# A two-layer decoder step on one core: first four weight units worked in halves, high-part products ahead, the next three units in idle banks, and GpSimd's squares after the low parts of x

## Chip, cores and metric

One core of a Trainium2 chip runs the whole step as one program. The metric is device time in microseconds; lower is better. Three runs of the kernel before had a median of 1188.85 us (1187.78 to 1189.05).

## What is computed

The reference is one inference step of a decoder trunk of two layers for 256 prompt rows and 8 decode rows (264 columns side by side, `N`). The change touches only the first matrix product of the first layer, `swiglu(rmsnorm(x), wi, wo)`:

```python
def rmsnorm(x, g):
    y = xf * lax.rsqrt(jnp.mean(xf * xf, axis=-1, keepdims=True) + EPS)
    return (y * g).astype(x.dtype)

def swiglu(x, wi, wo):
    gt, up = jnp.split(x @ wi, 2, axis=-1)
    return (jax.nn.silu(gt) * up) @ wo

x = x + 0.5 * swiglu(rmsnorm(x, w['ffn1_norm'][i]), w['ffn1_wi'][i], w['ffn1_wo'][i])
```

After it follow a Mamba-2 mixer, further SwiGLU blocks, shared K/V, window attention and gated embeddings, all through the same weight stream.

## The kernel before

**Units.** All weights are cut into units of 128x1024 fp32 (512 KB), numbered from 0 through the whole network, which go through a ring of four slots (`RING`). For each unit SP loads `raw`, ScalarE (ACT) copies it to `whi` in fp32r (the high part), VectorE (DVE) subtracts to get `wlo` (the low part), and TensorE (PE) makes for each of the unit's 8 tiles three products into one PSUM bank, `split_products`: `whi` by `xh`, `whi` by `xl`, `wlo` by `xh`, so 24 matmuls of 128x264 a unit. `xh` and `xl` are the high and low part of the input times the gain, one tile of each for every 128 rows of the model. The row factor 1/rms isn't in them: DVE multiplies it in when it takes a finished bank (`take`, L1623), after the squares of x have been summed (`sums`, L544, a plain fp32 matmul), rooted on ACT (`root`, L1154) and inverted on DVE (L1617, `row_factor`).

**What orders the work.** Each engine has its own program, written out by hand, and waits on counting semaphores: `first_hi`, `hi_ready`, `first_lo`, `lo_ready` (halves and units split), `xh_ready`, `xl_ready` (tiles of x), `unit_used` (units that PE has finished, four ahead at the start), `a_free` (banks that DVE has taken, also four ahead), `first_part` and `first_sum` (sums of squares of GpSimd and DVE). SP loads unit u into its slot only when `lo_ready` shows that unit u - 4 has been split. ACT splits unit u + 4 only when `unit_used` shows that unit u has been used. So of a slow step in one engine, everything queued behind it is late too.

**The beginning, stage `f1i0`.** PE runs 30 matmuls on zeros (`warm_up`, L504). x comes in four pairs of tiles (`x_pair`), units 0 and 1 in halves (four tiles each), units 2 and 3 whole. PE works units 0 and 1 side by side two tiles at a time, each tile with all its three products, then unit 2, the sums, unit 3. From unit 4 on each unit waits for its bank out of four (`unit_a`). GpSimd (POOL) squares three tiles of x and adds them as soon as x lands, ACT squares the other five (L1136), DVE adds those (L1794) and joins both (L1796). SP loads units 2 and 3, then, behind `lo_ready`, units 4 and 5, three tables (`cs`, `convs`, `vs`: 802.5, 384 and 143 KB), and units 6 and 7. The rest of the stage is a loop of four units a turn, in which `gate` and `up` take banks, ACT makes `silu`, and `hidden`, `round_h` and `low_h` make the high and low part of the hidden tile.

Of the kernel before, what the change touches and what calls it, by code (L numbers as in the profile page):

```python
# [22 lines left out]
P = 128  # L23
# [16 lines left out]
WARM = 30  # L40
# [90 lines left out]


# [36 lines left out]
def trunk_kernel(nc, weights, xT, g1, pT, cst, vec, convst, ssm0, kcT, vc_in, ck, cv,  # L169
# [3 lines left out]
    with ExitStack() as ctx:  # L173
# [77 lines left out]
        half_landed = [sem(f"half_landed{s}") for s in range(2)]  # L251
# [193 lines left out]
        def _(sp):  # L445
            sp.dma_start(gain0, g1).then_inc(gain_landed, 16)
            for h in range(4):
                sp.dma_start(x[:, 2 * h:2 * h + 2, :], xT[:, 2 * h:2 * h + 2, :]).then_inc(x_pair[h], 16)
                if h == 0:
                    for u in range(2):  # L450
                        sp.dma_start(raw[:, u, 0:HALF], weights[u, :, 0:HALF]).then_inc(half_landed[u], 16)
                if h == 1:
                    for u in range(2):
                        sp.dma_start(raw[:, u, HALF:UNIT], weights[u, :, HALF:UNIT]).then_inc(raw_landed[u], 16)
            for u in range(2, 2 * RING):
                if u >= RING:
                    sp.wait_ge(lo_ready, u - RING + 1)
# [39 lines left out]
        def _(pe):  # L497
# [78 lines left out]
            def first_units(stage, b_wait, rh=xh, rl=xl):  # L576

                if stage == "f1i0":
                    pe.wait_ge(a_free, A0[stage] + 2)
                    for h in range(KT // 2):  # L580
                        for j in range(2):
                            if h == 0:
                                pe.wait_ge(first_lo, j + 1)
                            if h == KT // 4:
                                pe.wait_ge(lo_ready, j + 1)
                            for k in (2 * h, 2 * h + 1):
                                pe.wait_ge(xl_ready, XREADY[stage] + k + 1)
                                mm = split_products(bank[j][:, 0:N], j, k, rh[:, k, :], rl[:, k, :], k == 0, k == KT - 1)
                    mm.then_inc(unit_used, 2)
                    unit_a(stage, 0, 2)  # L590
                    sums(stage)
                    unit_a(stage, 0, 3)
                    return
# [3 lines left out]
                for j in (2, 3):  # L597
                    unit_a(stage, 0, j, b_wait, rh=rh, rl=rl)

# [381 lines left out]
            ffn_in("f1i0", None)  # L981
# [109 lines left out]
        def _(act):  # L1091
# [64 lines left out]
            def ffn_in(stage, out, ffn, aside=None, late_work=False, spread=None):  # L1156
# [9 lines left out]
                if stage == "f1i0":  # L1166
# [3 lines left out]
                    act.preload_act_table(ACT.Silu)  # L1170
                else:
# [5 lines left out]
                ahead(stage, 0, 2)  # L1177
                round_h(0, 0)
                silu(0, 1)
                ahead(stage, 0, 3)  # L1180
# [56 lines left out]
            for m in range(KT):  # L1237
                if m % 2 == 0:
                    act.wait_ge(x_pair[m // 2], 16)
                act.activation(xh[:, m, :], x[:, m, :], ACT.Copy, scale=gain0[:, m:m + 1]).then_inc(xh_ready, 1)  # L1240
                if m == 1:
                    for u in range(2):
                        act.wait_ge(half_landed[u], 16)
                        act.activation(whi[:, u, 0:HALF], raw[:, u, 0:HALF], ACT.Copy).then_inc(first_hi, 1)
                if m == 3:
                    for u in range(2):
                        act.wait_ge(raw_landed[u], 16)
                        act.activation(whi[:, u, HALF:UNIT], raw[:, u, HALF:UNIT], ACT.Copy).then_inc(hi_ready, 1)
            round_unit(*unit(0, 0, 2))
            for m in range(POOL_SQUARES, KT):  # L1250
                square_x(m)
            round_unit(*unit(0, 0, 3))
# [317 lines left out]
        def _(dve):  # L1570
# [48 lines left out]
            def take(dst, stage, j, i=0):  # L1619

                dve.wait_ge(unit_used, U0[stage] + j + 4 * i + 1 + RING)
                src = bank[sin_bank(j) if stage == "sin" else QUERY_BANK[j] if stage == "q" else (A0[stage] + j) % 4]
                dve.tensor_tensor(dst, src[:, 0:N], rstd[:, :], ALU.mult).then_inc(a_free, 1)  # L1623

            def ffn_in(stage, out, ffn, aside=None, late_groups=0, spread=None):
# [16 lines left out]
                if stage == "f1i0":  # L1642
                    ahead(stage, 0, 0)
                row_factor(stage)
# [4 lines left out]
                ahead(stage, 0, 1)  # L1649
# [35 lines left out]
                with dve.Fori(SPREAD_AT[-1] + 1 if late_groups else 1, 2 * FT // RING) as i:  # L1685
# [90 lines left out]
            for m in range(KT):  # L1776
                if m % 2 == 0:
                    dve.wait_ge(x_pair[m // 2], 16)
                dve.wait_ge(xh_ready, m + 1)
                dve.scalar_tensor_tensor(out=xl[:, m, :], in0=x[:, m, :], scalar=gain0[:, m:m + 1], in1=xh[:, m, :].bitcast(F32),  # L1780
                                         op0=ALU.mult, op1=ALU.subtract).then_inc(xl_ready, 1)
                if m == 1:
                    for u in range(2):
                        dve.wait_ge(first_hi, u + 1)
                        dve.tensor_tensor(wlo[:, u, 0:HALF], raw[:, u, 0:HALF], whi[:, u, 0:HALF].bitcast(F32), ALU.subtract).then_inc(first_lo, 1)
                if m == 3:
                    for u in range(2):
                        dve.wait_ge(hi_ready, u + 1)
# [790 lines left out]
```

## Time and profile before

| | us |
|---|---|
| median of 3 runs | 1188.85 |
| lowest, highest | 1187.78, 1189.05 |
| the profiled execution's own time | 1188.74 |
| its span in the trace | 1186.9 |
| PE busy | 1174.9 (99%) |
| DVE busy | 866.4 (73%) |
| ACT busy | 698.7 (59%) |
| POOL busy | 246.2 (21%) |

The span is what the trace covers; the time of a run is 1.84 us more in this execution. A row of a timeline has the start in us from the span's start, the busy time, the engine and the operation, and in brackets how long the engine had been idle ahead of it and what ended that. "x2" is two instructions merged in one row.

### The profile page before, as it was taken

How to read it: one execution, taken by the hardware profiler on the slowest of the kernel's cores; microseconds unless marked ns; L12 is line 12 of the kernel's file. 1: busy time of each engine (PE TensorE's matmuls, PEld its weight loads, DVE VectorE, ACT ScalarE, POOL GpSimd, SP SyncE). 2: the span in 40 equal slices, each digit the busy share in tenths (PEclk: the TensorE clock that was granted, in tenths of full speed). 3: DMA queues.
4: the chain of work that ended last, by engine and by line, in shares of the span. 5: the costliest groups of instructions: out<-in, count | busy, mean ns of one | idle time of the engine just before them, and what ended most of it. 6: DMA issues, size and time to landing. Idle time of an engine off the chain costs nothing.

```text
span 1186.9 us, 26623 instructions
## 1 busy us (share of the span) xinstructions
PE 1174.9 (99%) x9823; PEld 1153.3 (97%) x9823; DVE 866.4 (73%) x1377; ACT 698.7 (59%) x1149; POOL 246.2 (21%) x352
## 2 busy tenths in 40 slices
PE   9999999999999999999999999999999999999998
PEld 8999999999999899999999999999999899999998
DVE  7766645999899858767745987788468777776447
ACT  6445435777786747555546765555368765444345
POOL 1000001422221202122344333232026310000001
PEclk9999999999999999999999999999999999999999
DMA  8765554755445375866886677656743346555552
GB/s 288 253 205 181 183 184 143 256 180 202 162 157 193 113 220 179 329 214 247 283 299 232 213 269 280 226 166 237 261 150 108 106 163 209 186 184 178 179 181 86
DMA packets 63297, 239.90 MB, mean 202 GB/s; under 512 B 7672, under 2 KB 9632, under 8 KB 58848
## 3 DMA queue, kind: packets, MB, share of 16 engines
q1 hardware_dynamic: 56880, 197.83, 49.8%
q0 software_dynamic: 6064, 40.66, 9.4%
q8 instruction: 41, 0.67, 0.2%
q10 hardware_dynamic: 288, 0.54, 0.2%
q14 instruction: 24, 0.20, 0.0%
HBM read 226.87 MB, written 13.39 MB: 202 GB/s over the span
## 4 chain that ended last, share of the span: by engine, by line
PE 87%; DVE 7%; ACT 3%; DMA 2%; issue 1%; POOL 0%; SPq 0%; DVEq 0%; ACTq 0%; POOLq 0%
PE bank L509 28%; PE bank L510 27%; PE bank L511 27%; DVE wlo L1576 1%; DMA raw<-weights 1%; DVE xact L1850 1%; DMA xact<-stat_rows 1%; ACT whi L1098 1%; DVE xl L1595 1%; PE bank L881 1%; PE bank L907 0%; PE bank L886 0%; ACT under L1494 0%; PE bank L687 0%; DVE zs L1976 0%
## 5 line engine op out<-in xcount | busy, mean ns | idle before, releaser
L1576 DVE TENSOR_TENSOR wlo<-raw,whi 128x1024 fp32r<-128x1024 f32 x367 | 456.0, 1246 | 236.9 <-ACT whi L1098 235.5
L509 PE MATMUL bank<-xh,whi 128*128 128x264 f32 x2008 | 576.5, 287 | 1.9 <-DVE zs L1623 0.8
L510 PE MATMUL bank<-xl,whi 128*128 128x264 f32 x2008 | 569.6, 284 | 0.0
L511 PE MATMUL bank<-xh,wlo 128*128 128x264 f32 x2008 | 569.3, 284 | 0.0
L1098 ACT ACTIVATE whi<-raw 128x1024 fp32r<-128x1024 f32 x367 | 385.5, 1054 | 242.4 <-PE bank L511 225.1
L509 PEld LDWEIGHTS bank<-xh,whi 128*128 128x128 f32 x2008 | 378.6, 189 | 5.0 <-DVE wlo L1576 1.8
L510 PEld LDWEIGHTS bank<-xl,whi 128*128 128x128 f32 x2008 | 378.8, 189 | 0.8
L511 PEld LDWEIGHTS bank<-xh,wlo 128*128 128x128 f32 x2008 | 376.9, 188 | 0.0
L509 PE MATMUL bank<-hh,whi 128*128 (+1 forms) x896 | 255.9, 286 | 1.8 <-DVE hl L1960 1.7
L511 PE MATMUL bank<-hh,wlo 128*128 (+1 forms) x896 | 255.0, 285 | 0.0
L510 PE MATMUL bank<-hl,whi 128*128 (+1 forms) x896 | 254.7, 284 | 0.0
L509 PEld LDWEIGHTS bank<-hh,whi 128*128 128x128 f32 x896 | 169.2, 189 | 2.7 <-issue 2.1
L510 PEld LDWEIGHTS bank<-hl,whi 128*128 128x128 f32 x896 | 169.1, 189 | 0.1
L511 PEld LDWEIGHTS bank<-hh,wlo 128*128 128x128 f32 x896 | 168.8, 188 | 0.0
L1164 ACT ACTIVATE hh<-gu 128x264 fp32r<-128x264 f32 (+1 forms) x88 | 37.4, 425 | 168.3 <-DVE gu L1635 168.3
L2204 POOL TENSOR_TENSOR sq<-sq 128x264 f32<-128x264 f32 x49 | 39.6, 808 | 448.4 <-ACT sq L1136 443.1
L1623 DVE TENSOR_TENSOR gu<-bank,rstd 128x264 f32<-128x264 f32 x192 | 82.1, 429 | 15.3 <-PE bank L511 12.8
L1640 DVE TENSOR_TENSOR hl<-gu,hh 128x264 f32 (+1 forms) x88 | 41.5, 472 | 28.7 <-ACT hh L1164 28.7
L2354 POOL TENSOR_TENSOR xact<-xact,da_bc 128x512 f32<-128x512 f32 x32 | 38.7, 1210 | 100.8 <-PE bank L511 100.8
L1850 DVE SCALAR_TENSOR_TENSOR xact<-under,vs,xact 128x256 f32<-128x256 f32 x96 | 47.3, 493 | 2.3
L1635 DVE TENSOR_TENSOR gu<-gu 128x264 f32<-128x264 f32 x88 | 44.1, 502 | 0.0
L2359 POOL TENSOR_TENSOR xact<-xact 128x512 f32<-128x512 f32 x20 | 29.1, 1457 | 59.9 <-PE bank L511 56.2
(335 smaller groups left out, 1007.2 us busy)
## 6 DMA issues: line engine op xcount, KB each, us to landing
raw<-weights SPq DMA_DIRECT2D x367, 512.0 KB, 3.5
under<-ssm POOLq DMA_DIRECT2D x8, 1024.0 KB, 7.1
xact<-ssm POOLq DMA_DIRECT2D x8, 1024.0 KB, 7.4
out_ssm_s<-xact POOLq DMA_DIRECT2D x8, 1024.0 KB, 6.0
xact<-dtx_rows POOLq DMA_DIRECT2D x5, 1024.0 KB, 10.7
zs<-dtx_rows POOLq DMA_DIRECT2D x2, 1024.0 KB, 14.1
x<-xT SPq DMA_DIRECT2D x4, 264.0 KB, 5.6
xact<-stat_rows POOLq DMA_DIRECT2D x2, 528.0 KB, 7.5
```

The costliest lines, as they stand in the source:

```text
L509: pe.matmul(out, whi[:, w, c], rh, start=start, stop=False)
L510: pe.matmul(out, whi[:, w, c], rl, start=False, stop=False)
L511: return pe.matmul(out, wlo[:, w, c], rh, start=False, stop=stop)
L1098: act.activation(whi[:, s, :], raw[:, s, :], ACT.Copy).then_inc(hi_ready, 1)
L1164: act.activation(dst, gu[:, 2 * p + 1, :], ACT.Copy).then_inc(hh_ready, 1)
L1576: dve.tensor_tensor(wlo[:, s, :], raw[:, s, :], whi[:, s, :].bitcast(F32), ALU.subtract).then_inc(lo_ready, 1)
L1623: dve.tensor_tensor(dst, src[:, 0:N], rstd[:, :], ALU.mult).then_inc(a_free, 1)
L1635: dve.tensor_tensor(gu[:, 2 * p + 1, :], gu[:, 2 * p, :], gu[:, 2 * p + 1, :], ALU.mult).then_inc(h_ready, 1)
L1640: dve.tensor_tensor(one(hl), gu[:, 2 * p + 1, :], one(hh).bitcast(F32), ALU.subtract).then_inc(hl_ready, 1)
L1850: dve.scalar_tensor_tensor(out=out, in0=xr[:, k:k + T], scalar=vs[:, V_CW + CT * k + c:V_CW + CT * k + c + 1], in1=out, op0=ALU.mult, op1= ...
L2204: pool.tensor_tensor(sq3[:, 0, :], sq3[:, 0, :], sq3[:, m, :], ALU.add).then_inc(sq_pair, 1)
L2354: pool.tensor_tensor(by_head(part), by_head(part), da_bc[:, 2 * k:2 * k + 2, 4 * q:4 * q + 4].unsqueeze(3).to_broadcast([P, 2, 4, 64]), AL ...
```

## The change

The first four units are all loaded, split and multiplied in halves, in this order: for tiles 0 to 3, units 0 and 1 two tiles at a time in turn, then units 2 and 3 four tiles each; then the same for tiles 4 to 7. Within such a piece (`first_piece`) PE makes all products of the high weights with `xh`, then those with `xl`, then those of the low weights, and waits only for what each of them reads. The sums come after unit 3. Units 4, 5 and 6 go to banks 5, 6 and 7, which are idle at this time (`first_bank`), without a wait for a taken bank; unit 7 waits for all four first banks. GpSimd's squares wait for all eight tiles of `xl`. The warming products are 22, not 30. ACT splits unit 6 ahead of the first `silu` and unit 7 ahead of the second. The first turn of PE's and DVE's loop is written out.

```diff
-WARM = 30
+WARM = 22
+def first_bank(n):
+    return n + 1 if 4 <= n < 7 else n % 4
...
+            load_x(0)
+            load_half(0, 0)
+            load_half(1, 0)
+            load_x(1)
+            load_half(2, 0)
+            load_half(3, 0)
+            load_x(2)
+            load_half(0, 1)
+            load_x(3)
+            for u in range(1, RING):
+                load_half(u, 1)
+            for u in range(RING, 2 * RING):
+                sp.wait_ge(lo_ready, u - RING + 1)
                 sp.dma_start(raw[:, u % RING, :], weights[u]).then_inc(raw_landed[u % RING], 16)
...
+            def first_piece(j, k0, n):
+                tiles = range(k0, k0 + n)
+                at = lambda k: slice(k * P, k * P + P)
+                for k in tiles:
+                    if k0 < KT // 2:
+                        pe.wait_ge(first_hi, j + 1)
+                    else:
+                        pe.wait_ge(hi_ready, j + 1)
+                    pe.wait_ge(xh_ready, k + 1)
+                    pe.matmul(bank[j][:, 0:N], whi[:, j, at(k)], xh[:, k, :], start=k == 0, stop=False)
+                for k in tiles:
+                    pe.wait_ge(xl_ready, k + 1)
+                    pe.matmul(bank[j][:, 0:N], whi[:, j, at(k)], xl[:, k, :], start=False, stop=False)
+                if k0 < KT // 2:
+                    pe.wait_ge(first_lo, j + 1)
+                else:
+                    pe.wait_ge(lo_ready, j + 1)
+                for k in tiles:
+                    mm = pe.matmul(bank[j][:, 0:N], wlo[:, j, at(k)], xh[:, k, :], start=False, stop=k == KT - 1)
...
+            def first_network():
+                pe.wait_ge(a_free, RING)
+                for half in range(2):
+                    k0 = half * KT // 2
+                    for k in (k0, k0 + 2):
+                        for j in range(2):
+                            first_piece(j, k, 2)
+                    for j in (2, 3):
+                        first_piece(j, k0, 4)
+                sums("f1i0")
+                for n in range(RING, 2 * RING):
+                    pe.wait_ge(lo_ready, n + 1)
+                    if n == 2 * RING - 1:
+                        pe.wait_ge(a_free, n + 1)
+                    for k in range(KT):
+                        mm = split_products(bank[first_bank(n)][:, 0:N], n % RING, k, ...)
+                    mm.then_inc(unit_used, 1)
...
+                    ahead(stage, 0, 2)
                 silu(0, 0)
-                ahead(stage, 0, 2)
+                ahead(stage, 0, 3 if stage == "f1i0" else 2)
...
+            low_half(0, 1)
+            low_half(1, 1)
+            low_pair(3)
+            low_half(2, 1)
+            low_half(3, 1)
...
             pool.memset(eps0, EPS)
+            pool.wait_ge(xl_ready, KT)
```

**DVE, from the split of tiles 4 and 5 of x to the reciprocal.** `wlo` 128x512 is half a unit, 128x1024 a whole one; `sq` is the chain of the squares. Before:

```order
L1780 SCALAR_TENSOR_TENSOR xl<-x,under,xh 128x264 [waits xh_ready,x_pair3]
L1780 SCALAR_TENSOR_TENSOR xl<-x,under,xh 128x264 [waits xh_ready]
L1576 TENSOR_TENSOR wlo<-raw,whi 128x1024 [waits hi_ready]
L1794 TENSOR_TENSOR sq<-sq 128x264 [waits sq_ready]
L1794 TENSOR_TENSOR sq<-sq 128x264 [waits sq_ready,dve_step] x3
L1796 TENSOR_TENSOR sq<-sq 128x264 [waits first_part,dve_step]
L1576 TENSOR_TENSOR wlo<-raw,whi 128x1024 [waits hi_ready] x2
L1617 RECIPROCAL rstd<-rstd 128x264 [waits std_ready]
```

And now:

```order
L1848 TENSOR_TENSOR wlo<-raw,whi 128x512 [waits hi_ready] x2
L1841 SCALAR_TENSOR_TENSOR xl<-x,under,xh 128x264 [waits xh_ready,x_pair3]
L1841 SCALAR_TENSOR_TENSOR xl<-x,under,xh 128x264 [waits xh_ready]
L1848 TENSOR_TENSOR wlo<-raw,whi 128x512 [waits hi_ready] x2
L1865 TENSOR_TENSOR sq<-sq 128x264 [waits sq_ready]
L1865 TENSOR_TENSOR sq<-sq 128x264 [waits sq_ready,dve_step] x3
L1867 TENSOR_TENSOR sq<-sq 128x264 [waits first_part,dve_step]
L1632 TENSOR_TENSOR wlo<-raw,whi 128x1024 [waits hi_ready] x2
L1673 RECIPROCAL rstd<-rstd 128x264 [waits std_ready]
```

The last two tiles of `xl` now stand behind two halves of `wlo`, and the two whole units behind the sum of squares are units 4 and 5, where they were 3 and 4.

**ACT, from the root to the second `silu`** (L1098 and L1143 split a unit, L1159 and L1204 are `silu`). Before:

```order
L1154 ACTIVATE rstd<-bank,under 128x264 [waits sums_done]
L1170 ACT_TABLE_LOAD
L1159 ACTIVATE gu<-gu 128x264 [waits a_free]
L1098 ACTIVATE whi<-raw 128x1024 [waits unit_used,raw_landed2]
L1164 ACTIVATE hh<-gu 128x264 [waits h_ready]
L1159 ACTIVATE gu<-gu 128x264 [waits a_free]
```

And now:

```order
L1199 ACTIVATE rstd<-bank,under 128x264 [waits sums_done]
L1215 ACT_TABLE_LOAD
L1143 ACTIVATE whi<-raw 128x1024 [waits unit_used,raw_landed2]
L1204 ACTIVATE gu<-gu 128x264 [waits a_free]
L1143 ACTIVATE whi<-raw 128x1024 [waits unit_used,raw_landed3]
L1209 ACTIVATE hh<-gu 128x264 [waits h_ready]
L1204 ACTIVATE gu<-gu 128x264 [waits a_free]
```

The split of unit 6, with its wait for the landing of unit 6, has moved ahead of the first `silu`.

**SP, up to the loop.** Now (before, the first wait for `lo_ready` stood behind the eleventh transfer, now behind the thirteenth, and what follows it is unchanged):

```order
L459 DMA raw<-weights 128x512 x3
L474 DMA raw<-weights 128x1024 [waits lo_ready] x2
L476 DMA cs<-cst 128x1605
L477 DMA zs<-convst 128x768
L478 DMA vs<-vec 128x286
L474 DMA raw<-weights 128x1024 [waits lo_ready] x2
```

What has moved is how far DVE must be for unit 4's load: `lo_ready` counts unit 0 only when its second half is split.

## Rows read from the trace of the kernel before

**Rows 1.** The page: span, busy time of PE, chain that ended last.

```profile
span 1186.9 us, 26623 instructions
PE 1174.9 (99%) x9823; PEld 1153.3 (97%) x9823; DVE 866.4 (73%) x1377; ACT 698.7 (59%) x1149; POOL 246.2 (21%) x352
PE 87%; DVE 7%; ACT 3%; DMA 2%; issue 1%; POOL 0%; SPq 0%; DVEq 0%; ACTq 0%; POOLq 0%
```

**Rows 2.** Stretches of PE: length, busy (products), granted clock, DMA share, GB/s.

```profile
7.66:17.96 10.30, 9.58 (x75) 1.00 0.96 349
17.96:21.66 3.70, 3.52 (x28) 1.00 1.03 404
21.66:24.56 2.90, 2.90 (x24) 1.00 0.62 218
30.36:1182.40 1152.04, 1146.41 (x9626) 1.00 0.59 200
```

**Rows 3.** Timeline of PE: warming, first product, sums, unit 4.

```profile
1.28 6.54 PE L504 MATMUL bank<-hh 128*128 128x264 f32 x30 [1.28 <-DVE hh L1774]
7.66 0.28 PE L509 MATMUL bank<-xh,whi 128*128 128x264 f32 x1
17.96 0.61 PE L544 MATMUL bank<-sq,under 128*128 128x264 f32 x2
21.66 0.36 PE L509 MATMUL bank<-xh,whi 128*128 128x264 f32 x1 [0.18 <-DVE gu L1623]
```

**Rows 4.** Pieces of the chain that ended last: start, us, what.

```profile
2.12 5.08 DMA raw<-weights
8.55 1.72 DVE xl L1780 x2
11.50 6.26 DMA raw<-weights
```

**Rows 5.** Timeline of ACT.

```profile
5.02 0.61 ACT L1244 ACTIVATE whi<-raw 128x512 fp32r<-128x512 f32 x1
7.22 0.63 ACT L1244 ACTIVATE whi<-raw 128x512 fp32r<-128x512 f32 x1 [1.59 <-DMA raw<-weights]
7.93 0.92 ACT L1240 ACTIVATE xh<-x,under 128x264 fp32r<-128x264 f32 x2
11.87 1.06 ACT L1098 ACTIVATE whi<-raw 128x1024 fp32r<-128x1024 f32 x1 [0.20 <-DMA raw<-weights]
16.55 1.06 ACT L1098 ACTIVATE whi<-raw 128x1024 fp32r<-128x1024 f32 x1 [1.10 <-DMA raw<-weights]
21.55 0.42 ACT L1159 ACTIVATE gu<-gu 128x264 f32<-128x264 f32 x1 [1.03 <-DVE gu L1623]
22.59 1.06 ACT L1098 ACTIVATE whi<-raw 128x1024 fp32r<-128x1024 f32 x1 [0.61 <-DMA raw<-weights]
```

**Rows 6.** Timeline of DVE.

```profile
4.85 1.85 DVE L1780 SCALAR_TENSOR_TENSOR xl<-x,under,xh 128x264 fp32r<-128x264 f32 x2 [3.62 <-ACT xh L1240]
6.62 0.68 DVE L1785 TENSOR_TENSOR wlo<-raw,whi 128x512 fp32r<-128x512 f32 x1
11.39 1.69 DVE L1780 SCALAR_TENSOR_TENSOR xl<-x,under,xh 128x264 fp32r<-128x264 f32 x4
14.15 1.82 DVE L1794 TENSOR_TENSOR sq<-sq 128x264 f32<-128x264 f32 x4
21.77 1.21 DVE L1576 TENSOR_TENSOR wlo<-raw,whi 128x1024 fp32r<-128x1024 f32 x1
```

**Rows 7.** Timelines of POOL and SP.

```profile
4.18 1.33 POOL L2211 TENSOR_TENSOR sq<-x 128x264 f32<-128x264 f32 x2 [3.21 <-DMA x<-xT]
5.59 0.82 POOL L2213 TENSOR_TENSOR sq<-sq 128x264 f32<-128x264 f32 x1
10.90 0.93 SPq L458 DMA_DIRECT2D raw<-weights  x2
14.29 3.64 SPq L458 DMA_DIRECT2D raw<-weights  x2
```

More of the change, by code:

```diff
@@ L250, in trunk_kernel @@
         x_pair = [sem(f"x_pair{h}") for h in range(4)]
-        half_landed = [sem(f"half_landed{s}") for s in range(2)]
+        half_landed = [sem(f"half_landed{s}") for s in range(RING)]
         first_hi = sem("first_hi")
@@ L576, in first_units @@
             def first_units(stage, b_wait, rh=xh, rl=xl):
[L578 to L593, printed above, removed]
                 unit_pair(stage, b_wait, stage != "f1i1", rh, rl)
@@ L598, in first_units @@
                     unit_a(stage, 0, j, b_wait, rh=rh, rl=rl)
+            def first_piece(j, k0, n):
[17 more added lines that the diff above has]
+                    mm = pe.matmul(bank[j][:, 0:N], wlo[:, j, at(k)], xh[:, k, :], start=False, stop=k == KT - 1)
+                if k == KT - 1:
+                    mm.then_inc(unit_used, 1)
[14 more added lines that the diff above has]
+                    for k in range(KT):
+                        mm = split_products(bank[first_bank(n)][:, 0:N], n % RING, k, xh[:, k, :], xl[:, k, :], k == 0, k == KT - 1)
+                    mm.then_inc(unit_used, 1)
+                with pe.Fori(2, 2 * FT // RING) as i:
+                    for j in range(RING):
+                        unit_a("f1i0", i, j)
             def first_units_p(stage, b_wait):
@@ L980, in _ @@
             warm_up()
[L981 removed]
+            first_network()
             stage_b("f1o0", FT, "sin")
@@ L1236, in _, with high_pair, high_half @@
             act.wait_ge(gain_landed, 16)
[L1237 to L1249, printed above, removed]
+            def high_pair(h):
+                act.wait_ge(x_pair[h], 16)
+                for m in (2 * h, 2 * h + 1):
+                    act.activation(xh[:, m, :], x[:, m, :], ACT.Copy, scale=gain0[:, m:m + 1]).then_inc(xh_ready, 1)
+            def high_half(u, h):
+                c = slice(h * HALF, h * HALF + HALF)
+                act.wait_ge(raw_landed[u] if h else half_landed[u], 16)
+                act.activation(whi[:, u, c], raw[:, u, c], ACT.Copy).then_inc(hi_ready if h else first_hi, 1)
+            high_pair(0)
+            high_half(0, 0)
+            high_half(1, 0)
+            high_pair(1)
+            high_half(2, 0)
+            high_half(3, 0)
+            high_pair(2)
+            high_half(0, 1)
+            high_pair(3)
+            for u in range(1, RING):
+                high_half(u, 1)
             for m in range(POOL_SQUARES, KT):
                 square_x(m)
-            round_unit(*unit(0, 0, 3))
             ffn_in("f1i0", "f1o0", 0)
@@ L1621, in take @@
                 dve.wait_ge(unit_used, U0[stage] + j + 4 * i + 1 + RING)
-                src = bank[sin_bank(j) if stage == "sin" else QUERY_BANK[j] if stage == "q" else (A0[stage] + j) % 4]
+                src = bank[sin_bank(j) if stage == "sin" else QUERY_BANK[j] if stage == "q" else
+                           first_bank(4 * i + j) if stage == "f1i0" and isinstance(i, int) else (A0[stage] + j) % 4]
                 dve.tensor_tensor(dst, src[:, 0:N], rstd[:, :], ALU.mult).then_inc(a_free, 1)
@@ L1643, in ffn_in @@
                     ahead(stage, 0, 0)
+                    ahead(stage, 0, 1)
                 row_factor(stage)
@@ L1648, in ffn_in @@
                     ahead(stage, 0, 0)
-                ahead(stage, 0, 1)
+                    ahead(stage, 0, 1)
                 hidden(0, 0)
```

54 lines of the change are left out of this document (26 added, 28 removed).

## Prediction

> **What bounds the kernel now.** I read the page first, for what the end hangs on: PE is busy 1174.9 of 1186.9 us and carries 87% of the chain that ended last [rows 1]. Then PE in stretches. From unit 4 on 24 products take 2.90 us, 0.121 us each, and from 30.36 to 1182.4 PE is busy 1146.41 of 1152.04 us [rows 2]. So behind the beginning nothing is to be had or lost by this change except as a shift: if unit n starts d earlier, where n is the first unit that no longer waits, the end comes d earlier. The whole question is what PE does ahead of that unit.
>
> Of PE's first 27 us: 30 warming products from 1.28 to about 7.66, then the first real product; the sums at 17.96, when 72 products (3 units) are done; unit 4 at 21.66 [rows 3]. 72 products at 0.121 are 8.7 us, and the stretch took 10.3, so 1.6 us are holes. From 17.96 to 21.66 stand the sums and unit 3's 24 products: 2.9 of 3.7 us, so 0.8 us for sums and the wait of unit 4 for its bank. What made the holes is in the chain [rows 4]: the load of unit 1's first half (ends 7.2), a pair of `xl` on DVE, and the load of unit 5 (ends 17.76), behind whose split on ACT the root is queued, and behind that the reciprocal. DVE and the transfers feed PE here, not PE itself.
>
> **Part 1, an earlier first product.** 22 warming products at 0.218 (6.54/30 [rows 3]) end at 1.28 + 4.8 = 6.1 us. Unit 0's first half is split at 5.02 + 0.61 [rows 5], so PE goes on at 6.1. Its first piece has six products; its last two want `wlo`, which DVE has at about 6.4: GpSimd no longer runs beside the first `xl` pair, and that pair cost 1.85 us beside it, 0.85 alone (half of 1.69 for four) [rows 6, 7]. The six end at 6.1 + 6 x 0.218 = 7.4. Then unit 1's first half is wanted, which lands at 7.2 and is split by 7.85 [rows 5]. So 0.5 us of hole, and the price of earlier start is bounded by a transfer: 12 products are done at about 8.9 (unit 1's low half at 8.6).
>
> Loads ahead: unit 1's half lands at 7.2 and unit 2 at 11.85 [rows 5], with 264, 256, 256, 264, 264 and 512 KB between, 0.66 us for each quarter MB. In the new order the pieces land at 7.9 (x pair 1), 8.55, 9.2 (units 2 and 3), 9.9, 10.5 (unit 0), 11.2 (x pair 3), 11.85, 12.5, 13.1 (units 1 to 3). ACT (0.61 a half, 0.46 an x tile) splits the second halves by 11.4, 13.0, 13.6 and 14.2. DVE (0.68 a half) has them by 12.1, 13.7, 15.2 and 15.9, with the last `xl` pair between the second and the third, at 14.5 [rows 5, 6]. PE, which from 9.3 on has 12 products of each unit's half ready to run, makes units 2 and 3's first halves until 13.4 and reaches each of the other pieces just after its `wlo`: unit 3 ends at 19.2. Before, it started at 18.21 and ended at 21.2. That is 2.0 us earlier, of which the sums, now behind it, take back 0.25 to 0.44.
>
> **Part 2, the sum of squares becomes late.** GpSimd starts at about 14.4. Its three squares (0.67 to 1.02; I take 0.7) and two additions (0.82) [rows 7] end at 18.3. DVE has two halves of `wlo` (1.36) and four additions (1.82 [rows 6]) in this time: 3.1 us alone. Alone, it waits for GpSimd until 18.3, joins at 18.7, and the sums at 19.2 wait for nothing. At the rate of the first `xl` pair beside GpSimd (half) it does 2.0 of 3.1 by 18.3, the rest by 19.4, joins by 19.8; sums 20.2. Behind the join DVE makes unit 4's `wlo` (1.21 [rows 6]): 19.9 or 21.0, and unit 4 starts at 20.0 or 21.1, against 21.66. These are the ends, gain 1.6 and 0.55; I take 21.1, since both GpSimd and DVE have two operands from SBUF here as in the row.
>
> The Trainium skill (GPSIMD Engine Reference, the table at its top) says that GpSimd shares its SBUF interfaces with VectorE and that instructions with two SBUF inputs contend; by that rule the move takes the cost away from `xl` and lays it on the chain of squares. The row of the first pair agrees.
>
> **Part 3, unit 6.** Here is what I think decides. Unit 4's load waits for unit 0's second low half: 12.1, where it was issued at 10.9 [rows 7]; unit 5's for unit 1's at 13.7 (11.5 [rows 4]); the three tables (1.33 MB) and unit 6's load stand behind it on SP. Unit 6 landed at 22.59, 4.8 us behind unit 5 [rows 4, 5]. If all is later as issued, unit 6 lands 1.3 later, 23.9; if the engines are full anyway, as late as before, 22.6. Unit 4's load took 5.6 us though the queue was draining, so mostly the issue counts: I take 23.5. Now ACT holds the first `silu` behind unit 6's split. From the landing: split 1.06, `silu` 0.42, `hidden` and `gate` on DVE 0.8, `wlo` of unit 6 1.21 [rows 5, 6], so 3.5 us and 0.1 to PE: 27.1 (26.2 to 27.5). The other bound for unit 6 is unit 4's start plus two units: 26.9 (25.8). Before, it started at 21.66 + 5.8 = 27.46. So the gain that remains is about 0.35 us (0 to 1.6). What the idle banks save (0.18 idle and the slower start of the row at 21.66, about 0.4) is in these numbers: unit 4 doesn't wait for the reciprocal any more.
>
> Behind unit 6: unit 7 lands 1.25 later, is split at about 26, needs four taken banks (DVE at 28) and its `wlo` (29.3), and PE wants it at 30.0: covered by 0.7 us. The unrolled turns, the banks and the later `k_old` transfer lie beside PE and cost nothing while that cover lasts.
>
> **The sum.** 1186.9 - 0.35 = 1186.55 of span, and 1.84 around it: 1188.4 for the profiled execution, which stood 0.11 below the median of 1188.85. So 1188.5.
>
> **Rivals.** (A) *Data and DVE come early.* The load that ended at 7.2 had been issued at 2.12 and took 5.08 us [rows 4], 0.7 us being what such a piece needs. If it lands at 6, as its size would allow, all pieces follow 0.7 to 1.2 earlier, and DVE isn't slowed in the squares: unit 4 starts at 19 to 19.8, unit 6 at 24.8 to 25.6, 1.9 to 2.7 us earlier: 1186.2 to 1187.0. Against it: before would be no such gainer, its first product being bound by the warming, and the row of contention is plain.
>
> (B) *Nothing remains*: unit 6 lands at 23.9 or later, `silu` late, 27.5 or more: 1188.9 to 1189.6.
>
> (C) *Slower: the clock.* The warming ran at 0.218 a product, 264 columns at 1.2 GHz, until shortly before 7.66, and products run at 0.121, 2.4 GHz, behind it [rows 2, 3]; what PE had done was run without a hole for some 6 us. Now there is a hole of 0.5 us at 7.4. If it holds the rise off, each product costs 0.1 more. The first 12 are hidden by the feed. The sums' lateness hides 0.6 us, and unit 6's some more, so 15 slow products cost about nothing; from 40 slow products on (4.0 less 1.0 hidden, less 0.35 gained) it is over 1191.2. For it: nothing in the trace but the moment. Against: the holes of 0.5 and 0.3 us at 8 to 12 us left the clock at 1.00 [rows 2]. The Trainium skill (TensorE: Matmul & The Clock Gate, Part 1) says that the gate follows recent activity and that the moment of the rise varies between runs. By that rule a rise at about 8 us would be possible in this kernel too and would cost under 1 us, mostly hidden.
>
> **How the numbers follow.** A measurement of this kernel tells about 0.2%, 2.4 us, from no change. Forecast (gain 0 to 1.6) 0.56, (A) 0.22, (B) 0.16, (C) 0.06. Of (A) I count three quarters as over 2.4 us, since median runs differ by 0.6 either way and the feed may be better than I can read: faster 0.17, same 0.76, slower 0.07. The range takes (A)'s end and (B)'s with that 0.6: 1186.0 to 1190.0.
>
> **What would show it.** In the trace of the changed kernel: first product at 6.1; a hole at 7.4; `xl` tiles at 0.42; unit 3 done near 19.2; the join of squares at 18.7 to 19.8 and unit 4's start behind a `wlo`, not behind `gu`; ACT waiting for unit 6's transfer ahead of the first `silu`; unit 6's start at 27.1. I am wrong if unit 6 starts before 26 (its landing or the contention misjudged), or if the shift of unit 6 isn't the shift of the end.

## Result and the profile after

Over 22 runs each the changed kernel has a median of 1191.11 us (1189.02 to 1194.33), the kernel before 1189.09 (1187.78 to 1192.23): 2.0 us longer, ratio 1.0017, 95% interval 1.0011 to 1.0023. 14 of the 22 lie over 1190.5 us, of the kernel before 2 of 22. The forecast was 1188.5 in a range to 1190.0, so both sign and range failed.

The page of the changed kernel (first part, PE's line, chain by engine), to be read against [rows 1]:

```profile
span 1189.4 us, 26619 instructions
PE 1175.5 (99%) x9815; PEld 1153.7 (97%) x9815; DVE 869.1 (73%) x1379; ACT 698.8 (59%) x1151; POOL 247.7 (21%) x352
PE 86%; DVE 6%; ACT 3%; DMA 2%; issue 1%; SPq 0%; POOL 0%; DVEq 0%; ACTq 0%; POOLq 0%
```

It is bound as before; 2.5 us of span have come in somewhere. First the beginning, PE's timeline, then DVE's, then ACT's (against [rows 3, 5, 6]):

```profile
6.29 0.42 PE L610 MATMUL bank<-xh,whi 128*128 128x264 f32 x1
19.76 0.71 PE L560 MATMUL bank<-sq,under 128*128 128x264 f32 x2 [0.90 <-DVE sq L1867]
20.90 0.39 PE L525 MATMUL bank<-xh,whi 128*128 128x264 f32 x1 [0.42 <-DVE wlo L1632]
27.76 0.39 PE L525 MATMUL bank<-xh,whi 128*128 128x264 f32 x1 [0.78 <-DVE wlo L1632]
```

```profile
4.61 0.90 DVE L1841 SCALAR_TENSOR_TENSOR xl<-x,under,xh 128x264 fp32r<-128x264 f32 x2 [3.38 <-ACT xh L1288]
15.80 3.44 DVE L1865 TENSOR_TENSOR sq<-sq 128x264 f32<-128x264 f32 x4
19.27 0.43 DVE L1867 TENSOR_TENSOR sq<-sq 128x264 f32<-128x264 f32 x1
21.93 1.80 DVE L1673 RECIPROCAL rstd<-rstd 128x264 f32<-128x264 f32 x1
26.49 1.22 DVE L1632 TENSOR_TENSOR wlo<-raw,whi 128x1024 fp32r<-128x1024 f32 x1
```

```profile
19.70 1.06 ACT L1143 ACTIVATE whi<-raw 128x1024 fp32r<-128x1024 f32 x1 [3.00 <-DMA raw<-weights]
24.39 1.06 ACT L1143 ACTIVATE whi<-raw 128x1024 fp32r<-128x1024 f32 x1 [1.96 <-DMA raw<-weights]
25.36 0.40 ACT L1204 ACTIVATE gu<-gu 128x264 f32<-128x264 f32 x1
```

The first product comes at 6.29, not 7.66; unit 4 at 20.90, 0.8 us earlier than before. But unit 5 lands at 19.7, where it landed at 17.8 [rows 4], and unit 6 at 24.4, where it landed at 22.6 [rows 5]. Behind that landing stand its split, the first `silu`, `hidden`, `gate` and `wlo` at 26.49, and PE has unit 6 at 27.76, with 0.78 us of hole. The kernel before started it two units behind 21.66 [rows 3], at 27.56 in its trace. So at unit 6 the changed kernel is 0.2 us *behind*, from unit 7 on 0.3 (the first product behind a hole takes 0.1 longer, 0.39 for 0.28), and this 0.3 stays to 425 us.

The next two places are far from the change. The chain that ended last around 414 us, changed kernel, then kernel before, and the wait of PE behind it in the changed kernel (1.7 us in the kernel before):

```profile
414.42 10.11 DMA xact<-stat_rows
```

```profile
414.06 9.50 DMA xact<-stat_rows
```

```profile
PE bank L525 <- DVE hl L2030: 2.3, 1, 2.3
```

The mixer's group norm sends its row factors through memory and reads them back to all partitions (`stat_rows`). PE has other tiles to work on meanwhile, runs out of them, and stands until DVE has the ninth tile's low part. This hole has grown by 0.65 us. Then stretches of PE around the attention stage (length, busy, products, granted clock, DMA), changed kernel:

```profile
939.00:942.37 3.37, 3.12 (x74) 1.00 0.00 0
942.37:945.78 3.41, 3.41 (x23) 0.50 0.48 159
945.78:949.20 3.42, 3.42 (x30) 1.00 0.50 157
```

and what PE did ahead of it:

```profile
941.30 1.10 PE L778 MATMUL bank<-small,xact 128*64 128x4 f32 x32
```

Behind 32 products of four columns the clock fell from 2.4 to 1.2 GHz for 3.41 us: 1.2 us later from there on. The kernel before has 1.00 in these stretches. With 0.3 (beginning), 0.65 (hole), 0.1 (between 440 and 700 us), 1.2 (clock) and 0.2 (around the last sum of squares, at 1166 us) the 2.5 us of span are all placed. What runs had to tell was whether the last four belong to the change or to one execution.

### The profile page after: what moved, and what is told of

It is laid out like the page before. It is cut to its first block, busy times and chain, and to the rows that moved or that the text cites. A ratio compares the mean times of both kernels' runs of the same rounds, so it can differ in the third digit from the quotient of the medians.

```text
span 1189.4 us, 26619 instructions
## 1 busy us (share of the span) xinstructions
PE 1175.5 (99%) x9815; PEld 1153.7 (97%) x9815; DVE 869.1 (73%) x1379; ACT 698.8 (59%) x1151; POOL 247.7 (21%) x352
## 4 chain that ended last, share of the span: by engine, by line
PE 86%; DVE 6%; ACT 3%; DMA 2%; issue 1%; SPq 0%; POOL 0%; DVEq 0%; ACTq 0%; POOLq 0%
PE bank L525 27%; PE bank L526 27%; PE bank L527 27%; DVE wlo L1632 1%; DMA xact<-stat_rows 1%; DVE xact L1920 1%; DMA raw<-weights 1%; ACT whi L1143 1%; DVE xl L1651 1%; PE bank L926 1%; DMA x<-xT 0%; PE bank L952 0%; PE bank L931 0%; ACT under L1550 0%; PE bank L732 0%
## 5 line engine op out<-in xcount | busy, mean ns | idle before, releaser
L525 PE MATMUL bank<-xh,whi 128*128 128x264 f32 x1976 | 566.5, 287 | 2.2 <-DVE wlo L1632 1.4
L526 PE MATMUL bank<-xl,whi 128*128 128x264 f32 x1976 | 560.2, 283 | 0.0
L527 PE MATMUL bank<-xh,wlo 128*128 128x264 f32 x1976 | 559.7, 283 | 0.0
L1143 ACT ACTIVATE whi<-raw 128x1024 fp32r<-128x1024 f32 x365 | 383.4, 1054 | 239.2 <-PE bank L527 221.0
L525 PEld LDWEIGHTS bank<-xh,whi 128*128 128x128 f32 x1976 | 372.2, 188 | 5.1 <-DVE wlo L1632 3.6
L526 PEld LDWEIGHTS bank<-xl,whi 128*128 128x128 f32 x1976 | 372.4, 188 | 0.8
L527 PEld LDWEIGHTS bank<-xh,wlo 128*128 128x128 f32 x1976 | 370.6, 188 | 0.0
```

Of the source, the lines that this page charges most:

```text
L525: pe.matmul(out, whi[:, w, c], rh, start=start, stop=False)
L526: pe.matmul(out, whi[:, w, c], rl, start=False, stop=False)
L527: return pe.matmul(out, wlo[:, w, c], rh, start=False, stop=stop)
L1143: act.activation(whi[:, s, :], raw[:, s, :], ACT.Copy).then_inc(hi_ready, 1)
```

## Experiments

All are compared with runs of the kernel before on the same chip and beside them (medians 1188.85 to 1189.17). "Over" or "under the changed kernel" is against its median of 1191.11, which was not measured beside them. Each kernel has one profile. "Hole" is the gap between two products of PE at 426 us, 1.99 us in the kernel before and 2.62 in the changed one; a wait in a row is some 0.3 less.

### Is it the moment? Three shifts

```diff
+                    for _ in range(12):     # 26 in before_pad26
+                        pe.matmul(bank[7][:, 0:N], whi[:, 3, 0:P], xh[:, 0, :], start=True, stop=True)
                     unit_a(stage, 0, 3)
```

> The kernel before with 12 more products of 264 columns (whi slot 3 by xh, into bank 7, nobody reads them) ahead of unit 3. Their price is 12 x 0.121 = 1.45 us, less the 0.3 us that unit 4 waits anyway: everything behind the beginning is about 1.1 us later, as it is in the changed kernel when its attention stage starts. Theory M (the moment): the attention stage is then met by a fall of the granted clock to 1.2 GHz around 942 us, which costs 1.3 us more, so about 2.4 us over the kernel before, and PE's clock shows a stretch below 1.00 there. Theory S (shift only): 1.1 us over before, clock 1.00 throughout.

1189.93 us, 0.8 over before (ratio 0.9998 to 1.0016). Clock 1.00, hole 0.97 us.

> The same with 26 products: 3.15 less 0.3, so 2.8 us later. Theory M: the small products of the attention stage come at another moment again, so no fall of the clock around 942 us or one elsewhere; with none, 2.8 us over before, which is hardly more than with 12. Theory S: 2.8 us over before, 1.7 over the version with 12.

1191.52 us, 2.35 over before (1.0018 to 1.0036). Clock 1.00, hole 1.38 us.

> The changed kernel with 14 more products (whi slot 3 by xh, into bank 4, which nobody reads any more) ahead of unit 7: 1.7 us of PE work in a stretch where PE doesn't wait. Theory M: the small products around 940 us move away from the moment at which the clock fell, the fall goes, and of 1.7 us only 0.3 to 0.7 are seen over the changed kernel (median 1191.1), and the profile has a clock of 1.00 from 8 us to the end stage. Theory S: 1.7 us over the changed kernel, 1192.8.

1191.87 us, 0.8 over the changed kernel. Clock 1.00, hole 2.26 us.

Theory M in the form given wanted a fall in `before_pad12`, and 2.4 us over before: there was none, and 0.8. In the other two it wanted no fall, as theory S did, and there was none; but with one profile each this decides nothing, and the 0.8 us of `after_pad14` are nearer to M's 0.3 to 0.7 than to S's 1.7. Nor does a shift pass one to one to the end. In the profiles everything behind the beginning of `before_pad12` is 1.4 us later than in the kernel before, and the read too begins 1.4 us later (415.45), but it takes 8.49 us and not 9.50; in `before_pad26` it takes 7.32. PE's hole at 426 us ends with the read, so the shorter reads took up part of the shift; why they were shorter isn't known. What the moment of a change of clock depends on is better seen in the warming products. Two stretches of `before_pad26`, then the same of the kernel before, which does the same up to here (warming products alone; the clock's column has 1.00 in all four and doesn't show the rise, the number of products does):

```profile
2.00:4.00 2.00, 2.00 (x11) 2.00 (x11) 1.00 0.86 247
4.40:6.40 2.00, 2.00 (x17) 1.82 (x16) 1.00 0.84 264
```

```profile
2.00:4.00 2.00, 2.00 (x11) 2.00 (x10) 1.00 0.85 244
4.40:6.40 2.00, 2.00 (x11) 2.00 (x11) 1.00 0.78 243
```

The same warming reached 2.4 GHz at 4.1 us in one execution and 7.2 in the other (4.1 to 7.2 in the nine profiles with 30 warming products, 4.3 to 7.4 in the eleven with 22). So the moment at which the chip changes the clock isn't tied to the kernel's start, and whether a stretch of low work is answered by a fall can differ between executions of one kernel. The Trainium skill (TensorE: Matmul & The Clock Gate, Part 1) says that the moment varies from run to run, by about 500 ns either way. These traces agree that it varies, but over 3.3 us, and the measurement decides.

### What does the clock cost? Filling the hole

```diff
                 pe.wait_ge(lo_ready, u + 1)
+                if stage == "sout" and isinstance(kt, int) and kt == 8:
+                    for _ in range(10):
+                        pe.matmul(bank[0][:, N:512], whi[:, s, 0:P], xh[:, 0, 0:512 - N], start=True, stop=True, skip_group_check=True)
                 pe.wait_ge(hl_ready, hready)
```

In all filled kernels the turns of this stage's loop on PE are written out as well, so that one tile can be told from the others; no run has that part alone. In the two first ones the filling products start a sum in the idle columns, which changed the outputs (relative difference 0.39); no wait depends on values. Those with a b in their names, and the filled ones further below, add to these columns instead (`start=False`), which left the outputs as they were.

> The changed kernel with 10 products of 248 columns, read by nobody, in the hole at about 426 us, where PE waits 1.8 to 2.3 us for the low part of the mixer's ninth tile (that loop's turns are written out). They need 10 x 0.115 = 1.2 us, which the hole covers, and leave under 1.3 us of it. Theory M (falls of the granted clock behind low work of PE make up a good part of the difference): no fall near 428 us any more, the share of executions over 1190.5 us drops from about 6 in 10, and the median comes down by 0.5 to 1 us from 1191.1. Theory H (the length of the hole alone counts, whatever the clock does): the median stays within 0.3 us of 1191.1.

1189.50 us: 1.6 under the changed kernel, ratio to before 1.0001 (0.9992 to 1.0009); 1 of 12 runs over 1190.5.

> The same products in the kernel before, whose hole there was 1.7 us in the profile. Theory M: few falls to remove, so no change beyond 0.3 us, and up to 0.5 more where the hole is shorter than 1.2 us (it was 0.7 and 1.1 us in the two padded versions of this kernel). Theory H: the same. It serves to show what the filling costs by itself.

1188.75 us, ratio 1.0000 (0.9991 to 1.0008).

> The changed kernel with the ten filling products again, now added to the idle columns 264 to 511 of bank 0 instead of starting a sum there: in the first version the start of a sum in these columns spoiled the sum in columns 0 to 263, so its values weren't the reference's (no wait and no duration depends on values). Theory M: as the first version, 1189.5, and no fall of the clock near 428 us. Theory H: 1191.1.

1189.74 us, ratio 1.0005 (0.9996 to 1.0014); 2 of 11 runs over 1190.5. PE's wait is 0.8 us instead of 2.3, the read itself is as long as ever (9.85 us).

> The kernel before with the ten filling products added to idle columns at 426 us. If falls of the clock behind that hole cost the kernel before something too (a fifth of its executions lie over 1190.3 us), its median is 0.2 to 0.4 us under that of the kernel before and hardly an execution is over 1190.5; if not, they are equal.

1188.89 us (0.9994 to 1.0012), 2 of 11 over 1190.5: nothing to be had.

Work that nobody reads takes 1.4 to 1.6 us off the changed kernel (1.2 to 1.6 when each is set against the kernel before beside it) and nothing measurable off the kernel before. This fits theory M in its general form: the fills don't shorten the read, only PE's idleness ahead of its end. A profile that has the fall is that of `after_tables` (below), stretches of PE:

```profile
425.00:428.35 3.35, 1.54 (x12) 1.00 0.48 171
428.35:431.77 3.42, 3.42 (x18) 0.50 0.81 262
431.77:435.20 3.43, 3.43 (x30) 1.00 0.50 183
```

Over the twenty profiles: with a hole of 2.0 us or more, unfilled, the clock fell behind it in 3 of 8; with a shorter one in 0 of 6; filled in 0 of 6. The three falls made PE 1.5 to 1.7 us later. The fall at 941 to 946 us (1.2 us) is in 2 of 9 profiles made from the kernel before and in 3 of 11 made from the changed one, so nothing ties it to the change.

Every run, and not only the profiles shown, has its mean granted clock on record. In the twenty profiles a mean of 0.998 or less stands for a fall on the way, 0.999 or 1.000 for none. By this mark the unfilled changed kernel had a fall in 12 of 22 runs (mean 1192.4 us, the other ten 1189.8), its two filled versions in 4 of 23, the kernel before in 47 of its 160 runs beside the experiments (1190.3, the others 1188.8). So falls are more frequent in the changed kernel, and the fill removes that. But 2.6 us between the two groups of runs is more than one fall costs in a profile. What else is in the slow ones isn't shown; the holes at 820 us that two profiles have (1.9 us in `after_tables`, 1.0 in `after_start`) are a candidate.

### The beginning

```diff
-                if u == RING + 1:
+                if u == 2 * RING - 1:        # after_tables: cs, convs, vs behind unit 7
```

> The changed kernel with the loads of the three tables (cs, convs, vs, 1.33 MB) behind unit 7's load on SP, not ahead of unit 6's. Theory L (the landing of unit 6 is what PE waits for at 27.8 us): unit 6 lands 3.4 us earlier, around 21 us, its split isn't waited for, PE runs from 21.1 us (unit 4) without a hole, unit 6 starts at 26.9, not 27.8, and the end is 0.9 us earlier. Theory R (the reciprocal and the takes on DVE are the bound): unit 6's wlo stays behind hidden and gate at 26.5, unit 6 starts at 27.7 and nothing is gained.

1191.06 us (1.0005 to 1.0022). Unit 6 landed in time and started at 27.19, where the changed kernel had 27.76: 0.57 us, between the two theories, since unit 5 landed at 20.2 and held the root and the reciprocal. PE has 1.9 us of another hole at 820 us in this profile.

```diff
-            pool.wait_ge(xl_ready, KT)       # after_squares_early; in after_start: 4 instead of KT
```

> The changed kernel without GpSimd's wait for the low parts of x: it squares from about 4.2 to 10 us, as before. Theory C (DVE's chain of additions beside GpSimd and the join at 19.3 are what PE waits for before the sums and unit 4): additions take 1.8 us, not 3.44, the join is done by 18.1, PE's waits of 0.9 (sums) and 0.8 us (unit 4) go, unit 4 starts at 19.6 to 20, not 20.9; the first xl pair takes 1.85 us again, and the first pieces of PE come up to 0.9 us later, which unit 2 and 3 absorb. Unit 6 still starts near 27.7, behind its landing at 24.4, so the end gains 0 to 0.2 us. Theory G (GpSimd's place doesn't matter): no change anywhere.

1191.23 us (1.0003 to 1.0021). Timelines of DVE and of ACT:

```profile
15.23 1.83 DVE L1865 TENSOR_TENSOR sq<-sq 128x264 f32<-128x264 f32 x4
17.10 0.43 DVE L1867 TENSOR_TENSOR sq<-sq 128x264 f32<-128x264 f32 x1
```

```profile
23.98 1.06 ACT L1143 ACTIVATE whi<-raw 128x1024 fp32r<-128x1024 f32 x1 [1.56 <-DMA raw<-weights]
```

Theory C: the additions take 1.83 us, not 3.44, unit 4 starts at 20.25 without a wait, and unit 6 waits for its landing all the same. The gain ends there, as said.

```diff
                 row_factor(stage)
+                if stage == "f1i0":
+                    ahead(stage, 0, 2)       # after_start, with the two edits above
```

> The changed kernel with three edits to its beginning: GpSimd's squares wait for four tiles of xl, not eight (from 8.7 us); the tables are loaded behind unit 7; DVE splits unit 6 right behind the reciprocal, ahead of the takes. Theory F (feed): unit 4 starts by 19.8, unit 5 behind its landing (19.7 to 20.3 us) at about 22.7, unit 6 at 25.6 to 25.9, so 1.6 to 1.9 us earlier than in the kernel before (27.5), and the median is 1.6 to 2.1 us under the changed kernel's. Theory D (what is lost lies downstream, hole and clock, and takes what it takes): the beginning gains this, but the median stays over that of the kernel before.

1190.65 us (1.0001 to 1.0020). Unit 5 landed at 20.9 and started at 23.2, unit 6 at 26.25, 1.3 us ahead of the kernel before. Then PE stood 0.8 us for unit 7's low part, which DVE began at 28.93 behind the takes, and by 60 us the lead was 0.04 us. So theory F fell, and of theory D the half that stands is that the median stays over that of the kernel before: the beginning gave nothing that lasted, and more was lost downstream (hole 2.63 us, and 1.0 us at 820).

What the beginning costs by itself is better read from many profiles than from one pair, since it varies from one execution to the next. At one and the same product near 60 us the six profiles with the changed beginning as it is (`after`, the two fills, the two written-out versions, `after_turn2_fill`) lie between 0.6 us ahead of and 1.4 behind the profile of the kernel before, 0.3 behind on average; the six with the beginning of the kernel before lie 0.7 ahead to 0.1 behind, 0.3 ahead on average. So the change costs about 0.6 us there, and the profile of the kernel before was one of its later ones.

### Why is the hole longer?

Nothing at 414 us was changed, yet the unfilled kernels so far that were made from the changed one had holes of 2.62, 2.26, 2.09, 2.69 and 2.63 us, those from the kernel before 1.99, 0.97 and 1.38. But the padded kernels aren't like the others in this. Without them, and with `before_dve_turn` and `before_four_loads` from below, it is 2.51 on average (four profiles) against 1.79 (three), 0.7 us more. In 12 of the 14 unfilled profiles the hole is the read's length less 7.5 us (`after_pe_turn2` has 0.25 more, and in `before_pad26` the read began 1.6 us late), so what has to be explained is the read. What differs there in the trace is when the instruction queues fetch, 16 KB at a time on q8 and 8 KB on q14.

```diff
+                if stage == "f1i0":
+                    body(1)                  # before_dve_turn: DVE's first turn written out
+                    ...
+                    for j in range(RING):
+                        unit_a(stage, 1, j)  # before_pe_turn: PE's first turn written out
```

(The loops then begin one turn later. `after_pe_turn1` and `after_pe_turn2` write out one and two turns more than the changed kernel, `before_pe_turn2` two turns.)

> The kernel before with one part of the change alone: the first turn of DVE's loop in the first stage written out (12 more instructions in DVE's program, the same work in the same order). In all six profiles of kernels made from the changed one, the queue of instruction fetches has a fetch on q14 at 414 to 416 us, beside the read of stat_rows, and that read takes 9.6 to 10.4 us and PE's hole behind it is 2.1 to 2.7 us; in all four made from the kernel before, the q14 fetch isn't there, the read takes 7.3 to 9.5 and the hole is 1.0 to 2.0. Theory I (the length of a program moves its fetches, and these the read): if DVE's program is the one, this kernel shows a q14 fetch at 414 us, a hole over 2.1 us and a median of 1190 or more. Theory N (nothing to do with code length): hole 1.0 to 2.0, median 1189.0.

1189.60 us (0.9998 to 1.0016), hole 1.88, the read 9.38 us. An 8 KB fetch came at 419.6 in the read, where the kernel before has none; the 16 KB fetch stayed at 416.1.

> The same for PE: the first turn of its loop in the first stage written out (96 more instructions in PE's program, the same products). Theory I, if PE's program is the one: a q14 fetch beside the read of stat_rows, hole over 2.1 us, median of 1190 or more. Theory N, or DVE's program being the one: hole 1.0 to 2.0 us, median 1189.0.

1189.58 us (0.9994 to 1.0012), hole 2.34 us, read 9.84 us, and a fall of the clock behind it. The 16 KB fetch moved from 416.7 to 420.3. The hole is as theory I wanted it, the median isn't (1190 or more).

```diff
+                    sp.dma_start(raw[:, u, 0:HALF], weights[u, :, 0:HALF]).then_inc(late_half, 16)
+                    sp.dma_start(raw[:, u, HALF:UNIT], weights[u, :, HALF:UNIT]).then_inc(raw_landed[u], 16)
```

(In `before_four_loads`; ACT also waits for both first halves.)

> The kernel before with units 2 and 3 loaded in two halves each, so two transfers more on SP's queue, as in the changed kernel; ACT waits for both first halves. Theory Q (two more transfers move the queue's later ones against the engines): hole at 426 us of 2.1 us or more, median 1190 or more. Theory I: fetches and hole as in the kernel before (1.0 to 2.0 us), median 1189.0 to 1189.3, with unit 2's split up to 0.6 us later.

1189.06 us, hole 1.50: theory Q is out.

> The changed kernel with one more turn of PE's loop in the first stage written out (4654 instead of 4558 instructions in PE's program, the same products). In seven profiles of kernels made from the changed one the 16 KB fetch of instructions (q8) came at 417 to 422 us, at the end of the read of stat_rows, and the read took 9.6 to 10.4 us; with the kernel before it came at 414 to 417 and the read took 7.3 to 9.5; with PE's turn written out in the kernel before at 420, and the read took 9.8. Theory I (the fetch's place in time, set by the length of PE's program, makes the read longer): the fetch moves by whole steps of the program, and where it leaves the read (before 414 or behind 424 us) the read takes under 9.5 us and PE's hole is under 2.1 us; where it stays in its second half, 9.6 to 10.4 and a hole of 2.1 to 2.7. Theory N: read and hole as in the changed kernel wherever the fetch is.

1189.80 us (0.9997 to 1.0019). Fetch at 425.0, behind the read, which took 9.54 us; hole 2.06.

> The same with two more turns written out (4750 instructions). Theory I and theory N as for one turn.

1190.50 us (1.0005 to 1.0022). Fetch at 411.1, ahead of the read, which took 8.66 us; hole 1.41.

> The kernel before with two turns of PE's loop written out (4714 instructions). Theory I: read and hole follow the fetch's place, as above. Theory N: hole 1.0 to 2.0 us as in the kernel before, and the one hole of 2.3 us with one turn written out was an execution's chance.

1188.94 us (0.9991 to 1.0009). Fetches at 408.9 and 423.0; read 9.60, hole 2.08.

The read against the 16 KB fetch, all twenty profiles, by where the fetch began in the read of the same profile:

| fetch | profiles | read of stat_rows, us | mean |
|---|---|---|---|
| in the read's second half (419.5 to 423.0) | six from the changed kernel, before_pe_turn, before_pe_turn2 | 9.57 to 10.43 | 9.96 |
| in the read's first 3 us (413.9 to 418.4) | six from the kernel before, after_pad14 | 8.49 to 9.74 | 9.23 |
| outside the read, or at its very end | four from the changed kernel, before_pad26 | 7.32 to 9.54 | 8.87 |

Writing out one turn of PE's loop moved fetch and read of the kernel before into the first row; writing out one or two more moved those of the changed kernel out of it. And it holds within both families: with the fetch in the second half the mean is 10.04 us against 9.35 in kernels made from the changed one, and 9.72 (two profiles) against 8.89 in those made from the kernel before. That speaks for theory I. But `after_pe_turn1` missed its bound of 9.5 us by 0.04, the first two rows overlap, and each kernel has one profile. There is a rival besides: an 8 KB fetch on q14 began within 0.3 us of the read's start in all eleven profiles made from the changed kernel and in none of the nine others, and no run moved that one alone in the changed kernel. The place of the 16 KB fetch goes with 0.7 to 1.1 us of the read; that it is the cause isn't shown.

### Both together

> The changed kernel with both downstream costs treated: two turns of PE's loop written out (the 16 KB fetch was at 411 us then, outside the read of stat_rows, which took 8.7 us) and the ten filling products in the hole at 426 us. If the 2.0 us are the beginning (0.3), the longer hole and the falls of the clock, the median comes down to 1188.9 to 1189.5, no fall shows near 428 us and the read takes under 9.5 us. If something else in the changed kernel costs time, it stays at 1189.7 or more, as with either part alone.

1189.30 us, ratio 0.9998 (0.9989 to 1.0008), read 9.45 us, PE's wait there 0.4 us, no fall. With hole and fetch treated, the changed kernel is level with the kernel before. But `after_fill10` (1.0001) was that too by the fill alone, so what the fetch adds isn't shown.

> The same, with GpSimd's squares from the fourth tile of xl on (8.7 us) and not the eighth. Unit 4 starts at about 20 us, not 20.9, the wait of PE for the sum goes; unit 6 still waits for its landing (24.4 us) and starts at 27.5, 0 to 0.3 us earlier. So 0 to 0.3 us under the version beside it, 1188.7 to 1189.4; it is the candidate for one that is under the kernel before.

1192.38 us (1.0017 to 1.0034), all 12 runs over 1190.5: the opposite. Its profile (1195.23, the slowest of the twelve) shows where, ACT's timeline and stretches of PE:

```profile
26.64 1.06 ACT L1155 ACTIVATE whi<-raw 128x1024 fp32r<-128x1024 f32 x1 [3.84 <-DMA raw<-weights]
```

```profile
26.10:30.00 3.90, 0.28 (x3) 0.78 0.73 282
30.00:35.10 5.10, 5.10 (x23) 0.50 0.52 202
```

Unit 4 was early (it started at 20.28, the changed kernel's at 20.90), unit 6 landed at 26.6, PE stood 3.6 us and the clock fell from 28.3 to 35.1 us: from there on PE is 4.8 us behind the kernel before. In `after_turn2_fill`, which differs in the squares alone, unit 6 landed at 24.2. Part of the 2.5 us between them is in the traces. GpSimd, DVE and SP here, then SP in `after_turn2_fill`:

```profile
9.37 2.09 POOL L2294 TENSOR_TENSOR sq<-x 128x264 f32<-128x264 f32 x2 [8.41 <-DVE xl L1853]
12.58 2.28 DVE L1860 TENSOR_TENSOR wlo<-raw,whi 128x512 fp32r<-128x512 f32 x2
13.72 1.49 SPq L474 DMA_DIRECT2D raw<-weights  x2
```

```profile
12.09 2.15 SPq L474 DMA_DIRECT2D raw<-weights  x2
```

GpSimd squared from 9.4 to 14.3 us, beside DVE's split of the second halves. Two of these took 2.28 us there and 1.28 alone, so unit 0 was split later, unit 4's load went out 1.6 us later, and unit 6's 1.0 us later (16.68, where it was 15.71). In `after_start` the squares stand at the same place, and unit 4's load went out at 13.38. The other 1.5 us of unit 6's landing are open; the median says that something of the kind is the rule in this version. No version of the changed kernel beat the kernel before.

## Why the prediction was wrong, point by point

- **The step that failed** is "behind the beginning nothing is to be had or lost by this change except as a shift". I took a busy share of 1146.41 in 1152.04 us [rows 2] for proof that PE is insensitive. The holes left in it end with transfers and not with PE, and low work of PE costs twice, once as a wait and once as clock. What the 1.9 us between the means (2.0 between the medians) are made of can be estimated from the profiles: about 0.6 the beginning, 0.7 the longer hole, 0.2 around the last sum of squares (in 10 of 11 profiles made from the changed kernel and in no other), and 0.4 falls of the clock, which 12 of 22 runs had against 47 of 160, at about 1.5 us each. The fills took 1.4 to 1.6 us off the median, more than this last part: over half of the unfilled runs lie in the slower group, so the median stood in it. The unrolled turns, which the prediction put at nothing, are suspected of the longer read and not convicted.
- **Rival (C)** had the clock as the way to a slower kernel, but put it at the start and on PE's warming; there 22 products cost nothing (the rise came at 7.1 us). It had the clock right and the place wrong, with a chance of 0.06.
- **Part 1** held: first product 6.29 for 6.1. The hole at 7.4 wasn't there, since unit 1's half landed at 6.3 this time, and it gave nothing, as the next pieces set the pace.
- **Part 2** held: GpSimd from 14.32 (14.4), additions of 3.44 us beside it (1.83 alone in `after_squares_early`), join done at 19.7 (18.7 to 19.8), unit 4 at 20.90 (21.1).
- **Part 3** named the right bound, and its price was too small: unit 6 landed 1.8 us later than before, where I took 0.9 and had 1.3 as the end. Its load went out only 1.0 us later (15.25 for 14.29) and then took 9.1 us, where it had taken 8.3 [rows 5, 7]. Unit 6 started at 27.76 and not at 27.1: 0.3 us lost instead of 0.35 gained. Three slips of the prediction's own: the 1.6 us of holes that it reads out of PE's first 10.30 us are 0.7 in the row (9.58 busy) [rows 2]; unit 6 started at 27.56 in the kernel before, not 27.46; and the gain of up to 1.6 us doesn't fit the part's own bound for unit 6 (26.2, so 1.3).
- **Rival (A)** fell with the landing. **Rival (B)** (unit 6 lands at 23.9 or later, nothing remains) is what the beginning did, at 1188.9 to 1189.6; the filled kernels stand about there (1189.3 to 1189.7). The kernel itself, at 1191.11, is outside it.

## What to carry to other kernels

A kernel at 99% of one engine isn't safe from its few holes. List the holes and ask for each what ends it, whether the clock falls behind it, and whether its transfer meets anything that a change of code length moves (here suspected, not shown). At the start of a stream, follow the *landing* of the first load that waits for a free slot: work done earlier ahead of it only waits for it. And ask of every piece that is moved beside another engine which load waits for that engine: squares at 9 us held up the split that frees the first slot, and the version with them was the slowest. And where less than 0.2% matters, one profile on either side shows where time can go but not how often; the granted clock of every run tells more of that, and a filled hole tells a mechanism from an execution's chance.

## What the runs showed of the hardware

- The same warming products reached 2.4 GHz between 4.1 and 7.4 us after the start. A hole of PE of 2.0 us or more at 426 us was followed by 3.4 us at 1.2 GHz in 3 of 8 profiles, at a price of 1.5 to 1.7 us; 32 products of four columns, with PE busy, were followed by one in 5 of 20, at 1.2 us.
- Filling products that started a sum in columns 264 to 511 of a PSUM bank, beside the program's sum in columns 0 to 263, changed the program's outputs (relative difference 0.39, in both kernels); adding to these columns without a start didn't.
- Four additions of 264 columns on DVE took 3.44 us beside GpSimd's squares and 1.83 alone; two splits of 512 columns 2.28 and 1.28; a pair of `xl` 1.85 and 0.90.
- One read of 528 KB took 7.32 to 10.43 us in twenty profiles, 9.57 or more in all eight in which a 16 KB fetch of instructions began in its second half. That the fetch is the cause isn't shown.
